# The input projections as seven block products per pair of column blocks (Strassen form), in place of eight

## What is computed

```
proj = x @ w_in                     # (4096, 1024) @ (1024, 3328)
aq, ak, av, ag, bq, bk, bv, bg = split(proj)   # 512 each; bk, bv 128 each
ya = chunk_relbias_attention(aq, ak, av) * silu(ag)        # 8 heads, own chunk and 8 before
yb = sliding_window_sink_gqa(rope(bq), rope(bk), bv) * silu(bg)
h  = ALPHA * x + concat(ya, yb) @ w_out
h  = h + sigmoid(h @ w_gate) * (p @ w_ple)
out = layer_norm(h)
```

## Time and profile before

| | |
|---|---|
| median of three runs | 2696.57 us |
| the profiled execution | 2700.69 us, its span 2698.9 us |
| TensorE, of the span | 2584.9 us, 96% |
| VectorE | 1215.2 us, 45% |
| ScalarE | 1002.7 us, 37% |
| GpSimd | 354.6 us, 13% |
| mean traffic with HBM | 139 GB/s |

### The profile page before, as it was taken

One profiled execution on the slowest core, in us unless ns is written; L12 is line 12 of the kernel. 1 busy time (PEld: TensorE's weight loads), 2 busy tenths in 40 slices (PEclk: granted clock), 3 DMA queues, 4 the chain that ended last, 5 costly groups with the idle time before them and its releaser, 6 DMA issues. The chain is left out here.

```text
span 2698.9 us, 38010 instructions
## 1 busy us (share of the span) xinstructions
PE 2584.9 (96%) x14100; PEld 2257.2 (84%) x14100; DVE 1215.2 (45%) x2433; ACT 1002.7 (37%) x2091; POOL 354.6 (13%) x192
## 2 busy tenths in 40 slices
PE   7999999999999999999999999977999999999997
PEld 5888888998888888999989898875788888888886
DVE  5212136341111165158878786875433334334333
ACT  4111112231111122158878787764322322322222
POOL 2000000000000000000000000001344343443442
PEclk9999999999999999999999998998999999999999
DMA  6432237373322165385556547786444444444440
GB/s 198 150 119 75 82 88 136 134 239 119 131 86 82 62 120 150 121 280 162 167 170 215 167 127 241 249 226 183 111 118 108 131 116 109 120 120 117 118 111 34
DMA packets 365482, 377.06 MB, mean 140 GB/s; under 512 B 81560, under 2 KB 290600, under 8 KB 361640
## 3 DMA queue, kind: packets, MB, share of 16 engines
q1 hardware_dynamic: 364456, 374.61, 47.2%
q0 software_dynamic: 896, 0.80, 0.1%
HBM read 240.33 MB, written 136.07 MB: 139 GB/s over the span
## 5 line engine op out<-in xcount | busy, mean ns | idle before, releaser
L1345 PE MATMUL psum<-x_hi,w_hi 128*128 128x512 f32 x1344 | 525.1, 391 | 19.7 <-DVE x_lo L1049 17.5
L1345 PE MATMUL psum<-x_lo,w_hi 128*128 128x512 f32 x1344 | 525.1, 391 | 0.0
L1345 PE MATMUL psum<-x_hi,w_lo 128*128 128x512 f32 x1344 | 524.8, 390 | 0.0
L1345 PEld LDWEIGHTS psum<-x_hi,w_hi 128*128 128x128 f32 x1344 | 253.2, 188 | 72.6 <-issue 17.5
L1345 PEld LDWEIGHTS psum<-x_hi,w_lo 128*128 128x128 f32 x1344 | 253.2, 188 | 52.8
L1345 PEld LDWEIGHTS psum<-x_lo,w_hi 128*128 128x128 f32 x1344 | 253.1, 188 | 52.3
L722 POOL TENSOR_TENSOR y_raw<-y_two 128x512 f32<-128x512 f32 x32 | 41.2, 1286 | 1778.4 <-DMA y_two<-ya_d 1778.4
L1146 DVE CUSTOM_DVE_ANT_0 prob<-psum,bias 128x640 f32<-128x640 f32 (+4 forms) x256 | 199.2, 778 | 90.4 <-issue 90.0
L854 ACT ACTIVATE prob<-prob,small 128x640 f32<-128x640 f32 (+4 forms) x256 | 203.9, 797 | 65.2 <-DVE small L1146 61.1
L1243 DVE TENSOR_TENSOR y_lo<-y_raw,y_hi 128x1024 fp32r<-128x1024 f32 x32 | 39.2, 1225 | 397.6 <-ACT y_hi L883 397.6
L1345 PE MATMUL psum<-wo_hi,y_hi 128*128 128x512 f32 x512 | 203.2, 397 | 1.5 <-DVE wo_lo L1238 1.5
(11 more groups left out here) (163 smaller groups left out, 4854.0 us busy)
## 6 DMA issues: line engine op xcount, KB each, us to landing
qk_d<-stage_out SPq DMA_DIRECT2D x72, 512.0 KB, 2.7
w_raw<-in_w_in SPq DMA_DIRECT2D x20, 1024.0 KB, 5.5
v_d<-stage_out SPq DMA_DIRECT2D x64, 320.0 KB, 2.3
x_raw<-in_xT SPq DMA_DIRECT2D x32, 512.0 KB, 4.8
g_d<-stage_out SPq DMA_DIRECT2D x64, 256.0 KB, 2.0
bq_d<-stage_out SPq DMA_DIRECT2D x64, 256.0 KB, 4.1
ya_d<-y_a SPq DMA_DIRECT2D x128, 128.0 KB, 2.6
bq<-bq_d SPq DMA_DIRECT2D x32, 512.0 KB, 5.8
```

What stands on the lines that cost most here:

```text
L1345: return pe.matmul(dst, lhs, rhs, start=start, stop=stop)
```

## The change

The stage now goes over four groups of 1024 tokens, each as two token blocks of 512 (first index by k half, second by token half: X11 and X21 are the two k halves of the first 512 tokens, X12 and X22 those of the second). Sums of them are made once per group: T3 = X22 - X12, T2 = T3 + X11, T1 = X22 - T2 = X12 - X11, D2 = X21 - X22, T4 = D2 + T1. In the first group VectorE makes them; later GpSimd makes all but T4. X11, X21, X22 and T1 to T4 are split and kept for the group.

The feature columns but for the B keys are taken in ten pairs of 128-column blocks (`PAIRS`; the fourth and the eighth are B queries). A pair takes seven products, each of one 512-row half: 4 x 3 = 12 matmuls of 512. GpSimd makes the four mixed weight blocks from the four loaded ones. ScalarE splits the high part of weight block n + 5 at step n, VectorE the low part; seven slots hold them. Pairs use banks 0 to 2 and 3 to 5 in turn. Two products of a pair are copied to SBUF by ScalarE (snapshots), and VectorE makes the four results by seven additions: C11, U2, U3, U4, C22, C12, C21. From there a result goes the old way: high part, low part, store.

The values of one 128-token tile of both blocks (step m, four per group) take X11's product, X21's product and the product of T1 and X22: X11's serves both tiles. The B keys are made last in a group, in four products of 12 matmuls. The value weights are loaded and split once per group. The host lays x and the weights out in blocks, so that one partition's part of a 1 MB x block is 8 KB in one piece. The first head's queries are loaded when the last group's values begin, its keys and values after the last value product. Some buffers of stage A lie at other addresses.

The core of the diff:

```diff
--- before.py
+++ after.py
+GROUPS = 4
+GT = SEQ // GROUPS
+PAIRS = (("qk", 0), ("qk", 256), ("qk", 512), ("bq", 2048), ("qk", 768), ("g", 1024), ("g", 1280), ("bq", 2304), ("g", 1536),
+         ("g", 1792))
+BK = len(PAIRS)
+W_RING = 7
+W_AHEAD = 5
+OUT_AT = ((0, 0), (1, 1), (0, 1), (1, 0))
...
+                 "X21": x_raw_b[:, 0], "D2": x_raw_b[:, 0], "T4": x_raw_b[:, 0], "X22": x_raw_b[:, 1]}
+        X_OF = ("X11", "X21", "T2", "T1", "T3", "X22", "T4")
...
+                    eng.wait_ge(x_loaded[n], 16 * (g + 1))
+                a, b, op = "X22", "X12", ALU.subtract
+            elif name == "T2":
+                eng.wait_ge(x_split, x_at(g, "X11") + h + 1)
+                x_ready(eng, g, "T3", h)
+                a, b, op = "T3", "X11", ALU.add
+            elif name == "T1":
+                eng.wait_ge(x_split, x_at(g, "T2") + h + 1)
...
+            for g in range(GROUPS):
+                for a in range(BK):
+                    if a == 0 and g > 0:
...
+                        store_pair(g, a - 1, 3)
+                    if a + 1 < BK:
+                        load_w(g, a + 1, 3)
+                    if a == 0 and g > 0:
...
+                    store_pair(g, a, 0)
...
+                    store_pair(g, a, 1)
+                    if a < BK - 1:
+                        load_w(g, a + 2, 0)
+                        load_w(g, a + 2, 1)
...
+                    store_pair(g, a, 2)
+                store_pair(g, BK - 1, 3)
+                for m in range(4):
+                    if m == 0 and g + 1 < GROUPS:
+                        for name in ("X11", "X22", "X12", "X21"):
+                            load_x_block(g + 1, name)
...
+                a11, a12, s2, a21, s3, s4, a22 = (w_raw[:, i, :, :] for i in range(7))
...
+                pool.tensor_tensor(s3, a11, a21, ALU.subtract).then_inc(w_mixed, 1)
...
+                pool.tensor_tensor(a21, a21, a22, ALU.add).then_inc(w_mixed, 1)
...
+                pool.tensor_tensor(s2, a21, a11, ALU.subtract).then_inc(w_mixed, 1)
...
+                pool.tensor_tensor(s4, a12, s2, ALU.subtract).then_inc(w_mixed, 1)
...
+            mix_weights(0, 0)
+            mix_weights(0, 1)
...
             pool.wait_ge(setup, 3)
             for g in range(8):
                 for c in range(2):
                     pool.dma_start(trig_d[c, :, TB * g:TB * g + TB], swap[16 * g:16 * g + 16, c, :]
                                    ).then_inc(setup_stored, 16)
             pool.dma_start(bias_d[:, 0:384], bias_row[:, :]).then_inc(setup_stored, 16)
...
+            for g in range(GROUPS):
+                for a in range(2 if g == 0 else 1, BK):
+                    mix_weights(g, a)
+                if g + 1 < GROUPS:
+                    mix_weights(g + 1, 0)
+                    for name in ("T3", "T2", "T1", "D2"):
+                        for part in range(2):
+                            x_combine(pool, g + 1, name, part)
...
+            def snapshot(g, a, j):
+                act.wait_ge(prod_done, prod(g, "q", a, 3 * j) + 1)
+                if j == 0:
+                    snap_free(act, g, "q", a)
+                act.activation(snap[:, 4 * (a % 2) + 2 * j, :], psum[:, 3 * (a % 2) + 2 * j, :], ACT.Copy).then_inc(snap_done, 1)
...
+            def rope_hi(u, rope, row):
+                act.wait_ge(rope_done, rope + 1)
+                act.wait_ge(unit_stored[u % 2], stored_before(u))
+                act.activation(stage_out[:, u % 2, 0, :].bitcast(f32r), row, ACT.Copy).then_inc(unit_act, 1)
...
+            for g in range(GROUPS):
+                for a in range(BK):
+                    for i in range(7):
+                        if i in (0, 3):
+                            snapshot(g, a, i // 3)
+                        if a < BK - 1 or i < 4:
+                            w_hi(ring(g, a, i) + W_AHEAD)
+                        if a == 0 and i == 0 and g > 0:
+                            rope_hi(unit(g - 1, "k", 0), 10 * g - 2, snap[:, 3, :])
+                            x_block_hi(g, "T4")
...
+                            rope_hi(unit(g - 1, "k", 1), 10 * g - 1, snap[:, 4, :])
...
+                        rope = PAIRS[a][0] == "bq"
+                        if i in ((2, 5, 6) if rope else (1, 4, 5)):
+                            pair_out(g, a, ((2, 5, 6) if rope else (1, 4, 5)).index(i))
+                        if i == 6:
+                            pair_out(g, a, 3)
...
+                for m in range(4):
+                    for w in range(2):
+                        value_snapshot(g, m, w)
+                    for o in range(4):
+                        value_out(g, m, o)
...
+                act.wait_ge(prod_done, prod(g, "k", 0) + 1)
+                snap_free(act, g, "k", 0)
+                act.activation(snap[:, 4, :], psum[:, 6, :], ACT.Copy).then_inc(snap_done, 1)
+                if g + 1 < GROUPS:
+                    for name in ("X11", "T3", "T2", "X21", "T1", "X22"):
+                        x_block_hi(g + 1, name)
+                else:
+                    for j in range(2):
+                        rope_hi(unit(g, "k", j), 10 * g + 8 + j, snap[:, 3 + j, :])
...
+                for a in range(BK):
+                    for i in range(7):
+                        if a == 0 and i == 1 and g > 0:
+                            rope_unit(unit(g - 1, "k", 1), 10 * g - 1, 1, snap[:, 4, :])
+                        if a == 0 and i == 1 and g == 0:
...
+                            x_block(0, "T4")
+                        for name in ((), ("C11",), ("U2",), (), ("U3", "U4", "C22"), ("C12",), ("C21",))[i]:
+                            combine(g, a, name)
+                        if a < BK - 1 or i < 4:
+                            w_lo(ring(g, a, i) + W_AHEAD)
+                        if a == 0 and i == 0 and g > 0:
+                            dve.wait_ge(sum_done, summed(g - 1, "k", 1) + 1)
+                            rope_unit(unit(g - 1, "k", 0), 10 * g - 2, 0, snap[:, 3, :])
+                            x_block(g, "T4")
+                        if i in (1, 4, 5):
+                            pair_out(g, a, (1, 4, 5).index(i))
+                        if i == 6:
+                            pair_out(g, a, 3)
...
+                        if a == BK - 1 and i in (3, 5, 6):
+                            for k in range((0, 3, 6)[(3, 5, 6).index(i)], (3, 6, 8)[(3, 5, 6).index(i)]):
+                                v_weights_lo(g, k)
+                for m in range(4):
+                    for o in range(4):
+                        value_add(g, m, o)
+                        value_out(g, m, o)
...
+                if g + 1 < GROUPS:
+                    for name in ("X11", "T3", "T2", "X21"):
+                        x_block_lo(g + 1, name)
+                dve.wait_ge(snap_done, snapped(g, "k") + 1)
+                for j in range(2):
+                    dve.wait_ge(prod_done, prod(g, "k", 2 + j) + 1)
+                    dve.tensor_tensor(snap[:, 3 + j, :], snap[:, 4, :], psum[:, 6 + j, :], ALU.add).then_inc(sum_done, 1)
+                if g + 1 < GROUPS:
+                    for name in ("T1", "X22"):
+                        x_block_lo(g + 1, name)
...
+                    rope_unit(unit(g, "k", 0), 10 * g + 8, 0, snap[:, 3, :])
+                    rope_unit(unit(g, "k", 1), 10 * g + 9, 1, snap[:, 4, :])
...
+            for g in range(GROUPS):
+                for a in range(BK):
...
+                    for i in range(7):
+                        if i == 0 and a >= 2:
+                            pe.wait_ge(unit_done, unit(g, "q", a - 2, 3) + 1)
+                        elif i == 0 and g > 0:
+                            pe.wait_ge(unit_done, unit(g - 1, "v", 2 + a, 3) + 1)
+                        if i == 2:
+                            pe.wait_ge(snap_done, snapped(g, "q", a, 0) + 1)
+                        if i == 4:
+                            pe.wait_ge(sum_done, summed(g, "q", a, "U2") + 1)
+                        if i == 5:
+                            pe.wait_ge(snap_done, snapped(g, "q", a, 1) + 1)
+                        if i == 6:
+                            pe.wait_ge(sum_done, summed(g, "q", a, "U3") + 1)
+                        pe.wait_ge(w_split, ring(g, a, i) + 1)
+                        if a == 0:
+                            pe.wait_ge(x_split, x_at(g, X_OF[i]) + 2)
+                        feature_product(base + (0, 1, 0, 2, 0, 2, 0)[i], ring(g, a, i), X_OF[i])
...
+                    for w in range(2):
+                        token_product(bank + w, m, w, (("X11", 0),))
+                    if m == 0:
+                        pe.wait_ge(v_split, KT * g + KT)
+                    for w in range(2):
+                        pe.wait_ge(snap_done, snapped(g, "v", m, w) + 1)
+                        token_product(bank + w, m, w, (("X21", KH),))
...
+                        token_product(bank + 2 + w, m, w, (("T1", 0), ("X22", KH)))
+                for i in range(4):
+                    if i < 2:
```

(40 more changed lines are left out.)

805 lines of the change are left out of this document (447 added, 358 removed).

## The result

The changed kernel takes 2855.06 us as the median of four runs (2849.34 to 2857.5), the kernel before 2696.48 beside it (2695.4 to 2698.49): the ratio is 1.0584, 95% interval 1.0566 to 1.0602, so 158.6 us slower. The forecast was 2771, its range ended at 2840. The direction was right, the size was not: the loss is twice the one forecast.

A forecast was written before the change was run, and what follows sets the result against it. TensorE was taken to bound the first stage. New losses of 211.4 us, minus 28.4 old losses and 109 for the cut, gave +74: 2775 profiled, 2771 as median, range 2715 to 2840.

The forecast's parts named there:

- The cut: First stage: 84 matmuls for 96 per pair of column blocks and group, 480 wide matmuls less, 109 us saved.
- the snapshot behind a rotated pair: In eight rotated pairs, the next pair's first snapshot comes late behind ScalarE's rotation copy: 6.8 of 7.5 us lost per pair.
- U2 behind a group: At three group changes TensorE waits 13.1 us for VectorE's U2; with X21 and a snapshot 15.7 each, 47 us.
- the stores behind the x loads: Values part: stores queue behind 4.2 MB of loads, so TensorE waits 4.6 us for a snapshot, four times: 18 us.
- the start: Kernel start: products wait for X12's load and VectorE's sums, then trig issues delay weight mixes: 46.8 us, bounds 36 to 55.
- the end: End of the stage: the key's two rotations stand before stage A's first exponent on VectorE: 8 us.
- the clock: Matmuls run at half clock after 13 long pauses, 1.75 us each: 23 us, bounds 0 and 40.
- the start of the values: Four times, the last of eight value-weight splits on VectorE ends late and TensorE loses 2.1 us: 8 us.
- What would show it: Signs listed beforehand: matmul counts, last product near 1230 us, waits of about 7 and 13 us, unchanged GpSimd and VectorE durations.
- the first rival: GpSimd and VectorE block each other on SBUF operands in stage one: +56 us, 2827; chance 0.30.
- The cheap ends: Rival: 8 KB descriptors load faster, the clock mostly holds, the start takes 36: +30, 2727; chance 0.15.
- The buffers take up VectorE's lag: Rival: weight slots and banks absorb VectorE's delay, so rotated-pair and group-change losses and their clock go: 2645; chance 0.10.

## Why the prediction was wrong

**Right, and shown.** The cut: 480 matmuls, 109 us. The bound: TensorE, with plain pairs at 0 (between 148.66 and 213.60 us 23 products took 64.9 us, for 62.7 and one slow restart). The places of all waits: the snapshot behind a rotated pair 7.4 for 6.8, U2 behind a group, X21, the stores behind the x loads, the start, the end 8.9 for 7.7.

Some of this is luck. At the start the parts are 32.8, 1.9 and 10.4 us of waits for 38.7, 1.1 and 7.0; TensorE went on at 49.54 us as forecast (49.6), but part of the way there was slow running, which stands under the clock. (The forecast's 24.6 for X12 is 1.0 more than its own 2.8 + 5.2 / 0.25; VectorE's first sum started at 24.40.) And the 2.1 at the start of the values was worked out for the last of the eight splits, where the run without GpSimd's work has no wait at all; its 2.36 is another wait, told below.

Of "What would show it", the 3 x 1184 matmuls and the places of the waits came out. The last product near 1230 us (it was 1314), the waits of about 13 (15 to 16), and VectorE without idle time in a rotated pair (18.56 of 21.36 us busy from 214.77 on, its idle time in waits for ScalarE and for products) did not. GpSimd's adds at 2.39 and VectorE's operations at 0.69 did not either: that is the first rival, though not by its sign, gaps of the length of an add. There are no gaps; the operations themselves are longer. One reading was loose: of the earlier trace rows two lines of ScalarE wait for a DMA too (12.0 and 23.6 us), not only for a matmul or for VectorE; no term hung on it.

**The step that failed** is the price of GpSimd's work beside VectorE's, put at nothing in the sum: its adds at 2.39 us, its mixes at 1.29 and VectorE's operations at 0.69 and 1.22, as if each engine had SBUF to itself. Exclusion was held as a rival at 0.30 with the argument that no row decided. The runs show it: taking GpSimd's work away gives 65 us back (36 for the sums of x, 29 for the mixes), for a price of 56 (36 and 20). The 36 is right; the 29 is not only the rotated pairs that the price was made of, but also 10 us at the start of the values and 3.7 at 97 us. The Trainium skill (SBUF — State Buffer, Who interferes with whom) states the rule, and this case's runs agree: 1.22 us become up to 3.42 on one engine, 2.39 become 3.35 on the other, operations with a PSUM input stay at 0.68, and moving the adds onto the late engine makes the kernel faster. With the rival taken as the forecast the sum was 2827, 28 below what was measured. The argument against it was only the lack of a row in a kernel in which GpSimd has nothing to do in this stage; that is no evidence against, and the weights should have been the other way about.

**The second is the clock**, 23 for 49; its miss of 26 is near the 28 that even the rival's sum lacked. The price of 1.75 us was near (1.9 in the run with filled pauses, 2.2 in the mean of the changed kernel), the count was off: 13 restarts were charged, 22 are in the trace. The missing ones are three at X21, which the exclusion made long (8.7 for 1.6), one at the start, one of 6.6 behind a value store, and four behind shorter waits in the values and at U2. Exclusion is not what made the count: without GpSimd's work the three at X21 are gone, and there are still 22 restarts and 50 us, with others behind the waits of 2.36 us and for value stores. Rows of before told of both outcomes behind some 2.3 us; I charged none of those.

**At the start of the values** 8.4 was forecast and 19.2 measured, in two waits each time. The first, 2.36 in all four groups and in every kernel, is for the fourth of the eight splits, which I did not count: VectorE's list makes them in threes, between the sums of the last pair. Its timeline:

```profile
906.97 2.30 DVE L1195 TENSOR_TENSOR vw_lo<-v_raw_a,vw_hi 128x640 fp32r<-128x640 f32 x3
...
914.70 2.30 DVE L1195 TENSOR_TENSOR vw_lo<-v_raw_a,vw_hi 128x640 fp32r<-128x640 f32 x3
```

TensorE goes on at 915.67, behind the first of the second three. That this order is the cause is read from the trace; no run changed it. The second wait, up to 3.23, is for the last split, and the run without GpSimd's work took it away: it belongs to the first step. (In the two kernels that lack the rotation as well, 1.1 to 1.2 us of it come back in some groups.)

**The rest** closes. The waits and the clock in the run without GpSimd's sums and mixes, beside the forecast's terms:

| term | forecast | without GpSimd's work | changed kernel |
|---|---|---|---|
| rotated pairs | 60 | 58 | 70 |
| changes of group | 47 | 42 | 72 |
| start of the values, splits | 8.4 | 9.4 | 19.2 |
| value stores behind loads | 18.4 | 15.0 | 16.1 |
| start | 46.8 | 41.7 | 45.3 |
| end | 7.7 | 8.9 | 8.9 |
| clock and not assigned | 23 | 57 | 59 |
| together | 211 | 232 | 291 |

The clock makes up the 19 us between 2771 and 2790.

The other rivals are out. "The cheap ends" wanted the clock to hold and the start to take 36. "The buffers take up VectorE's lag" said 2645: VectorE caught up in the plain pair, but U2 and the next snapshot are needed within a product, as the prediction had it; with only the order changed the waits moved and shrank (48 us for 70), they did not go.

## What to carry to other kernels

A cut in matmuls that moves work to the other engines is judged at the few places where one product of slack has to cover a fixed list of theirs; sum those, then ask which two engines are in SBUF together there, and let an engine that was idle before count as a slower copy of the late one, not as help. Count the restarts at the low clock one by one, and give a wait that looks short a part of the price too, since a few more microseconds from elsewhere make it a long one. Where a written rule speaks against a change and the trace is silent, the rule is the forecast.

## What the runs showed of the hardware

- GpSimd and VectorE, each on two SBUF operands in float32: 128x1024 on VectorE 1.22 us alone, up to 3.42 beside a GpSimd add (2.04 to 2.96 in the mean of three groups of lines); on GpSimd 2.39 alone and 3.35 in company; the 128x512 mix 1.29 alone, 1.36 to 1.51 in the mean. Two splits and two adds together take 6.6 us, for 7.2 one after the other. Operations of VectorE with one PSUM operand: 0.683 with and 0.684 without GpSimd's work.
- The granted clock stood at 1.00 behind waits of 1.17 to 1.37 us; of those between 2.0 and 4.0 some left it at 1.00 (2.31, 3.23) and some did not (2.00, 2.40). In the kernel with the other order around the rotation two waits of 1.91 and 1.93 us did both (0.52 in the 2 us from 457.46, 1.00 from 853.81). Behind 7.42 us 13 matmuls ran at the lower level, behind the 15.07 at 385.43 only 7: the longer wait did not cost the longer stretch.
